# Expert gate and up weights of a one-core encoder step: eight two-row transfers per expert, or two whole matrices

## What is computed

```python
def expert_block(args):          # 128 token slots and the expert they belong to
    rows, e = args
    xb = hp[rows]
    a = xb @ p['moe_w_gate'][e]  # 1024 -> 512
    v = xb @ p['moe_w_up'][e]    # 1024 -> 512
    return (jax.nn.silu(a) * v) @ p['moe_w_down'][e]   # 512 -> 1024
```

## Time and profile before

| | us |
|---|---|
| median of three runs | 1191.03 (1185.85 to 1195.0) |
| span of the profiled execution | 1191.2 |
| TensorE busy | 1106.2 (93%) |
| gate and up products, L1154 | 299.4 |
| down products, L1183 | 150.9 |
| idle of TensorE before L1154 and L1183 | 20.0 and 11.5 |
| first gate product to last down product | 625.1 to 1143.7 |

### The profile page before, as it was taken

How to read it: one execution, slowest core, us unless ns; L and a number is a source line. 1 busy time by engine, 2 the same in 40 slices (tenths; PEclk the granted TensorE clock), 3 DMA queues, 4 the chain that set the end, 5 groups by cost and what they waited for, 6 DMA issues and landing times.

```text
span 1191.2 us, 17482 instructions
## 1 busy us (share of the span) xinstructions
PE 1106.2 (93%) x7024; PEld 538.6 (45%) x7024; DVE 439.0 (37%) x1048; ACT 249.8 (21%) x488; POOL 113.7 (10%) x202
## 2 busy tenths in 40 slices
PE   6999999999998999999989999989999998998645
PEld 3666666767754564555553333323333332332211
DVE  3589998380047762323352210101011100110017
ACT  3300012102553872322120000000000000000007
POOL 0000000000055000000320010000100100010016
PEclk9999999899999999999989999999999999999978
DMA  7121124004001104000978999999999999999868
GB/s 292 36 98 38 35 73 73 1 1 123 14 21 65 83 1 168 36 35 36 371 257 276 411 415 357 413 413 414 377 410 411 405 415 412 411 411 414 346 234 326
DMA packets 73491, 271.84 MB, mean 228 GB/s; under 512 B 10625, under 2 KB 15425, under 8 KB 65345
## 3 DMA queue, kind: packets, MB, share of 16 engines
q1 hardware_dynamic: 67200, 252.61, 55.4%
q0 software_dynamic: 6048, 17.83, 3.8%
q10 hardware_dynamic: 160, 0.26, 0.1%
HBM read 251.18 MB, written 23.55 MB: 231 GB/s over the span
## 4 chain that ended last, share of the span: by engine, by line
PE 59%; DVE 17%; DMA 8%; SPq 8%; ACT 4%; issue 3%; POOL 0%; POOLq 0%; DVEq 0%; ACTq 0%
PE psA L1154 17%; PE psB L1183 9%; DVE psC L1708 7%; SPq L571 6%; PE psA L1004 4%; PE psB L1004 4%; DMA arena<-in_w_down 4%; PE psA L680 3%; PE psB L680 3%; PE psC L805 3%; PE psA L824 2%; DMA arena<-in_w_up 1%; DMA arena<-hn_rows,ints 1%; PE psC L1139 1%; DVE arena L1708 1%
## 5 line engine op out<-in xcount | busy, mean ns | idle before, releaser
L1154 PE MATMUL psA<-arena 128*32 128x512 f32 x2688 | 299.4, 601 | 20.0 <-DMA arena<-in_w_up 18.2
L1154 PEld LDWEIGHTS psA<-arena 128*32 128x32 f32 x2688 | 86.8, 111 | 215.2 <-issue 211.9
L1183 PE MATMUL psB<-arena 128*32 128x512 f32 x1344 | 150.9, 599 | 11.5 <-DMA arena<-in_w_down 11.5
L680 PE MATMUL psA<-arena 128*128 128x360 f32 (+1 forms) x384 | 122.6, 478 | 11.4 <-DVE arena L1585 11.4
L2157 DVE TENSOR_TENSOR arena<-psA,arena 128x512 f32<-128x512 f32 x21 | 14.5, 692 | 317.1 <-ACT arena L1524 317.1
L680 PE MATMUL psB<-arena 128*128 128x360 f32 (+1 forms) x384 | 121.9, 477 | 0.0
L680 PEld LDWEIGHTS psA<-arena 128*128 128x128 f32 x384 | 73.7, 194 | 55.6 <-issue 14.1
L680 PEld LDWEIGHTS psB<-arena 128*128 128x128 f32 x384 | 74.3, 194 | 44.4 <-issue 2.4
L1183 PEld LDWEIGHTS psB<-arena 128*32 128x32 f32 x1344 | 42.8, 110 | 104.1 <-issue 102.0
L1708 DVE SCALAR_TENSOR_TENSOR psC<-arena,params,psC 128x1024 f32<-128x1024 f32 x70 | 89.8, 1283 | 0.0
L1524 ACT ACTIVATE arena<-psA 128x512 f32<-128x512 f32 x21 | 12.5, 597 | 307.1 <-PE psA L1154 307.1
(11 more groups left out here) (437 smaller groups left out, 1184.9 us busy)
## 6 DMA issues: line engine op xcount, KB each, us to landing
arena<-in_w_gate SPq DMA_DIRECT2D x128, 512.0 KB, 13.7
arena<-in_w_up SPq DMA_DIRECT2D x128, 512.0 KB, 16.7
arena<-in_w_down SPq DMA_DIRECT2D x64, 1024.0 KB, 15.0
arena<-in_w_cm SPq DMA_DIRECT2D x16, 512.0 KB, 3.6
arena<-expert_rows SPq DMA_DIRECT2D x16, 512.0 KB, 10.5
arena<-in_xT SPq DMA_DIRECT2D x8, 544.0 KB, 10.0
arena<-in_w_out SPq DMA_DIRECT2D x1, 4096.0 KB, 12.6
arena<-in_x_rows SPq DMA_DIRECT2D x8, 512.0 KB, 7.7
```

The costliest lines, as they stand in the source:

```text
L680: mm = te.matmul(AB[j % 2][:, 512 * b:512 * b + hi - lo], wring[:, j % 4, k * P:(k + 1) * P], xn[:, k, lo:hi], start=(k == 0), stop=(k == ...
L1154: mm = te.matmul(psA[tile, at:at + FF], xgT[:, k, tile], w[o % RG][:, k, :], start=(k == 0), stop=(k == KT - 1))
L1183: mm = te.matmul(psB[tile, n * 512:(n + 1) * 512], hT[:, k * P + c * TW:k * P + c * TW + TW], w, start=(k == 0), stop=(k == 3))
```

## The change

A part is one whole matrix: `GC` is 2, part 0 is gate and part 1 is up, each with all 8 rows of a partition. The transfers, the semaphores and the order of the products follow.

```diff
-RG, RD, GC, DC = 3, 2, 4, 2
+RG, RD, GC, DC = 3, 2, 2, 2
+GK = 8
...
-GK, DK = KT // GC, 4 // DC
+DK = 4 // DC
+
+
+GU_PARTS = [(m, slice(GK * h, GK * h + GK)) for h in range(KT // GK) for m in range(2)]
+assert len(GU_PARTS) == GC
...
-                r, ks = n % RG, slice(c * GK, c * GK + GK)
-                for w, src in ((wg[r], a["w_gate"]), (wu[r], a["w_up"])):
-                    sp.dma_start(w[:, ks, :], src[ds(e, 1), :, :].rearrange("o (p k) n -> (o p) k n", k=KT)[:, ks, :]
-                                 ).then_inc(s_wgu[r][c], 16)
+                r, (m, ks) = n % RG, GU_PARTS[c]
+                w, src = ((wg[r], a["w_gate"]), (wu[r], a["w_up"]))[m]
+                sp.dma_start(w[:, ks, :], src[ds(e, 1), :, :].rearrange("o (p k) n -> (o p) k n", k=KT)[:, ks, :]
+                             ).then_inc(s_wgu[r][c], 16)
...
-                        te.wait_ge(s_wgu[o % RG][part], 32 * (o // RG + 1))
-                    for k in range(part * GK, part * GK + GK):
-                        for w, at in ((wg, 0), (wu, FF)):
-                            for c, o in enumerate(QUADS[q]):
-                                tile = slice(c * TW, c * TW + TW)
-                                mm = te.matmul(psA[tile, at:at + FF], xgT[:, k, tile], w[o % RG][:, k, :],
-                                               start=(k == 0), stop=(k == KT - 1))
+                        te.wait_ge(s_wgu[o % RG][part], 16 * (o // RG + 1))
+                    m, ks = GU_PARTS[part]
+                    for k in range(ks.start, ks.stop):
+                        for c, o in enumerate(QUADS[q]):
+                            tile = slice(c * TW, c * TW + TW)
+                            mm = te.matmul(psA[tile, m * FF:(m + 1) * FF], xgT[:, k, tile], (wg, wu)[m][o % RG][:, k, :],
+                                           start=(k == 0), stop=(k == KT - 1))
```

## The result

The changed kernel takes 1256.2 us in the median of four runs (1247.8 to 1263.1), the kernel before 1191.7 beside it: a ratio of 1.056 (95% interval 1.052 to 1.060). It is 65 us slower; the forecast was 16 us slower, with 1228 as the top of the range.

The account below looks back on a forecast made before the run. It took DMA engines and TensorE as both full in the expert stage, the gather not yet on the path. Turns +31, clock +9, given back -24 made +16 us on 1191.2: 1207 us, range 1181 to 1228.

Parts of the forecast that it names:

- What bounds the kernel, and the slack of the gather: Expert stage: DMA engines and TensorE both full; a gather has 11.8 us, lands in 9.9 in the median, slack 1.9.
- Matmuls in another order, at 0: Gate and up products on TensorE: same 2688 instructions, all eight k steps of gate into one bank, cost 0.
- Issue at 0: SP's issue of weight DMAs, 64 of 2 MB instead of 256 of 512 KB: not on the path, nothing won.
- Transfer time, 12 us: Gate and up weight transfers: 16 KB pieces run faster than 4 KB ones, 9 to 18 us saved, 12 taken.
- Grain, 2 us: Behind an expert's last byte half of the products is left instead of a quarter: 2 us, once, in the last block.
- Turns on the DMA engines: Each scattered or gathered row waits for one weight packet; landing 14.3 to 15.9 us, waits of 2.6 in 12 blocks: +31.
- The clock, 9 us: TensorE's lower granted clock after waits for gathered rows: 12 x 0.75 = 9 us added.
- What is given back, 24 us: TensorE's present DMA losses: the 19.9 us before the last block go, part of the last block's 15.1 stays; 24 back.
- 11 us kept in the last block: Of the last block's 15.1 us lost to DMA, 11 stay: 6.2 from a down slot, 2 of grain, some rest.
- Gathers that don't slow: Rival on the DMA engines: only the transfer saving acts, 1181 us, or 1175 at the higher rate; chance 0.28.
- gathers that slow a little: Rival: landing 13 us in the median, 1.2 us of waiting in 12 blocks, no clock loss, 1185 to 1193; chance 0.20.
- Late release that starves the DMA: Rival: weight slots fall free 3.5 us later and the DMA idles in seven blocks, +12, 1203 us; chance 0.07.

Follow-up runs that it names:

- experiment 1: The changed kernel with each gather issued one step earlier, ahead of the scatter it stood behind: 1185.6 us, ratio 0.996 to the kernel before.
- experiment 9: The kernel of experiment 2 (4 KB pieces, whole matrices) with each gather issued one step earlier: 1195.9 us, ratio 1.004 to the kernel before.
- experiment 2: The changed kernel with each matrix brought by four DMAs in 4 KB pieces, order, wait and release kept: 1195.5 us, ratio 1.006 to the kernel before.
- experiment 3: The changed kernel with each matrix brought by two DMAs in 8 KB pieces, the rest kept: 1194.3 us, ratio 1.003 to the kernel before.
- experiment 6: The changed kernel with each gather ahead of its scatter in the queue, but issued at the same moment: 1186.9 us, ratio 0.995 to the kernel before.
- experiment 5: The changed kernel with each matrix in four 512 KB DMAs over every fourth partition, pieces still 16 KB: 1194.2 us, ratio 1.004 to the kernel before.
- Experiment 7: The changed kernel with four useless products on TensorE before the transposes of each block from the fifth on: 1228.4 us, ratio 1.030 to the kernel before.

## Why the prediction was wrong

**What bounds the kernel, and the slack of the gather.** Right. The 11.8 us hold: a median landing of 15.7 goes with waits of 4.1 in the mean.

**Matmuls in another order, at 0.** Right: 13.94 us per block in both kernels.

**Issue at 0.** Right; no wait of TensorE grew from it.

**Transfer time, 12 us.** Right in kind, a little large. Full slices went from some 413 to 423 GB/s, and experiments 1 and 9 put it at some 9 us where it can reach the end. In the changed kernel it reached nothing, because the rows set the pace.

**Grain, 2 us.** Too small: experiment 2 keeps grain and order without the rest and is 4 to 11 us above the kernel before.

**Turns on the DMA engines: the step that failed, by its size.** The mechanism, one packet for one whatever its size, is shown by the order of the packets and by experiments 1, 2, 3 and 6, and the landing was close (14.3 to 15.9 forecast, 15.7 measured). I turned it into 12 blocks of 2.6 us, 31 us; it was 16 of 4.1, 65.8 us. Two things were wrong. The per-block price took the lower end, on the ground that a third of the turns would meet down's 8 KB pieces. Counted over the 18 pairs of scatter and gather, SP's pieces met were 79 of 8 KB and 210 of 16 KB per pair, 27%, but nine of the 18 pairs met next to nothing but 16 KB. And the number of blocks was taken from the share of bytes, as if a block waited or didn't according to what it met; in fact the gate and up pieces in any mixed pair were enough to pass 11.8 us.

Two terms of the count were missing too, and they work against each other. A row slot that holds no token moves nothing but takes its turn, and so do POOL's semaphore writes: each pair shows 288 packets in POOL's queue, whether 153 or 242 of them carry a row, which is 18 turns an engine and not 16. And some of SP's turns are semaphore writes, which cost a row next to nothing (experiment 5). The packets of the earlier trace rows are therefore not all of 4 KB: SP's 0.86 MB are 210 pieces, beside 24 semaphore writes. Nor did equal counts show a change after every packet; that was a guess, and the times of the packets bear it out.

**The clock, 9 us.** The second step that failed by its size: 31.9 us in transposes and down products, 26.9 with the 5.0 that gate and up products gained. I read the price from waits of 2 to 3 us, where half were followed by 1.5 us. Now 15 of the 16 waits, all from 2.6 us up, were followed by slower work, and it covered the transposes, the down products or part of both. Experiment 7 gives 27.0 us back while the rows land as late as before.

**What is given back, 24 us.** Near, a little small: idle time fell by 26.0 us and gate and up products by 5.0, 31.0 in all. Of the 11 us kept in the last block 3.7 of waiting and 2.7 of clock were left. The sum in the forecast's terms is then +65.1 + 31.9 - 31.0 = +66, where it had +31 + 9 - 24 = +16.

**Rivals.** Gathers that don't slow, gathers that slow a little: excluded. Late release that starves the DMA: the dips to 231 GB/s look like it, but experiment 1 has the same release, full slices of 420 to 427 and no dip below 357 in the middle of the stage; the idling followed from TensorE's delay.

The range failed because both ends of the turn term were written down (0 and 4.1 us in all 19 blocks, which makes 78 us) and the upper one wasn't kept in it. The cases that share a cause, long landings, many blocks and lost clock, come together, not as independent accidents.

## What to carry to other kernels

Before making a DMA's pieces larger, look at who else uses the DMA engines and how much slack it has: multiply its packets per engine, empty rows and semaphore writes included, by the time of one of your pieces. Put the transfer that something waits for ahead of the one that nothing waits for in the same queue; that cost a few lines here and turned a loss of 65 us into a gain of some 5. And price a wait on TensorE at more than its length: 16 waits of 4.1 us in the mean came with some 30 us of slower products besides.

## What was not expected of the hardware

- A DMA over 32 neighbouring partitions runs far below full rate on busy engines, 278 GB/s in the window shown and 214 to 258 in most slices; the same bytes in the same pieces over every fourth partition run at 418 to 427 GB/s in the fullest slices. Why was not tried.
- Semaphore writes and skipped rows of an indirect DMA each take a turn on their engine, though one lasts only 9 ns: 184 packets for 186 with a third of SP's being semaphore writes, and 288 packets per pair whatever the rows carried.
- The Trainium skill ("DMA: Bandwidth & Descriptors", "Queues, rings and completion order") lets an engine drain 9 to 17 descriptors of a queue before it turns to the next. Here it drained one: the counts are near equal with pieces of 4, 8 and 16 KB (249 packets against 241 in the last case), and there 240 of the 241 follow directly on a packet of the other queue.
